# A two-block network on one core: chain step over four tiles, depthwise convolution in 32x32 diagonals, projections shifted by a slot

## What is computed

```
a, gt = jnp.split(h @ w1 + b1, 2, axis=-1)
u = a * jax.nn.sigmoid(gt)
u = causal_depthwise_conv(u, w_dw, b_dw)          # 31 taps, each channel by itself
u = jax.nn.silu(layer_norm(u, ln_g, ln_b))
return u @ w2 + b2
```

```
r = heads(lerp(0) @ w_in[0]);  k = heads(lerp(1) @ w_in[1]);  v = heads(lerp(2) @ w_in[2])
gate = lerp(3) @ w_in[3]
...
sa = jnp.einsum('dbhij,dbhj->dbhi', s, a_t)
s = s * jnp.exp(lw_t)[..., None, :] + sa[..., None] * b_t[..., None, :] + v_t[..., None] * k_t[..., None, :]
y = jnp.einsum('dbhij,dbhj->dbhi', s, r_t)
```

## Time and profile before

| | us |
|---|---|
| three runs | 2366.45, 2372.62, 2377.30 |
| median | 2372.62 |
| the profiled execution, its own time | 2365.28 |
| its span, first to last instruction | 2363.6 |
| gate of the last tile to the layer norm (convolution) | 840 to 898.5 |
| slot -1 of the scan | 1359.6 to 1436.8 |
| slots 0, 1, 2, 3 | 82.8, 93.2, 89.8, 87.5 |
| slots 4, 5, 6, 7 | 78.3, 66.6, 71.5, 57.8 |

### The profile page before, as it was taken

One profiled execution on the slowest core, in us unless ns is written; L12 is line 12 of the kernel. 1 busy time (PEld: TensorE's weight loads), 2 busy tenths in 40 slices (PEclk: granted clock), 3 DMA queues, 4 the chain that ended last, 5 costly groups with the idle time before them and its releaser, 6 DMA issues. The chain is left out here.

```text
span 2363.6 us, 39368 instructions
## 1 busy us (share of the span) xinstructions
PE 2173.4 (92%) x16594; PEld 1613.0 (68%) x16594; DVE 1015.1 (43%) x2276; ACT 526.0 (22%) x933; POOL 320.4 (14%) x530
## 2 busy tenths in 40 slices
PE   4998999999999998999998889998998899879988
PEld 3887888878888776788853355565566666436656
DVE  4643543524430572578055444534434541140262
ACT  1112122311000101100023243424434431011151
POOL 0000000000000300000005624433432120000100
PEclk8999999999999999999998989999999799899999
DMA  8543347438854320677216746545544252112100
GB/s 358 221 178 143 143 143 209 112 143 318 301 227 162 115 80 36 254 302 295 92 47 246 230 129 163 153 117 143 162 108 119 51 158 83 73 76 107 71 1 18
DMA packets 127130, 359.73 MB, mean 152 GB/s; under 512 B 78696, under 2 KB 87144, under 8 KB 109424
## 3 DMA queue, kind: packets, MB, share of 16 engines
q1 hardware_dynamic: 93776, 209.90, 25.8%
q0 software_dynamic: 32608, 146.31, 18.2%
q10 hardware_dynamic: 576, 1.05, 0.1%
HBM read 340.36 MB, written 16.85 MB: 151 GB/s over the span
## 5 line engine op out<-in xcount | busy, mean ns | idle before, releaser
L306 PE MATMUL bank<-h,ring 128*128 128x256 f32 x2304 | 501.1, 381 | 5.1 <-DVEq L1113 3.3
L306 PEld LDWEIGHTS bank<-h,ring 128*128 128x128 f32 x2304 | 439.2, 191 | 69.5 <-DVEq L1113 4.9
L1968 PE MATMUL bank<-rw_feed 128*128 128x512 f32 x464 | 248.9, 645 | 18.7 <-DMA rw_feed<-in_rkvg 8.1
L1755 POOL DMA_DIRECT2D rw_feed<-rwkv_mixes x232 | 124.8, 538 | 464.5 <-PE bank L1968 456.5
L2282 DVE TENSOR_TENSOR rw_u<-bank,rw_lam 128x128 f32<-128x128 f32 x120 | 34.9, 291 | 294.9 <-PE bank L1887 289.5
L1023 PE MATMUL bank<-ffn_hidden,ring 128*128 128x256 f32 x704 | 152.4, 379 | 3.4 <-PEq L1049 3.4
L1023 PEld LDWEIGHTS bank<-ffn_hidden,ring 128*128 128x128 f32 x704 | 133.6, 190 | 22.2 <-issue 4.1
L527 PE MATMUL bank<-h,ring 128*128 128x256 f32 x640 | 143.1, 380 | 1.1 <-PEq L323 1.1
L1968 PEld LDWEIGHTS bank<-rw_feed 128*128 128x128 f32 x464 | 77.5, 195 | 88.6 <-issue 47.7
L527 PEld LDWEIGHTS bank<-h,ring 128*128 128x128 f32 x640 | 120.2, 190 | 20.2 <-issue 4.8
L139 PE MATMUL bank<-con 128*128 128x512 f32 x220 | 103.2, 621 | 32.3 <-DVE mod L133 14.4
(11 more groups left out here) (435 smaller groups left out, 3364.7 us busy)
## 6 DMA issues: line engine op xcount, KB each, us to landing
ring<-in_stream SPq DMA_DIRECT2D x79, 2048.0 KB, 8.1
rw_feed<-rwkv_mixes POOLq DMA_DIRECT2D x232, 256.0 KB, 3.1
next_w<-in_mod_stream POOLq DMA_DIRECT2D x24, 2048.0 KB, 9.9
ctx<-in_mod_rest POOLq DMA_DIRECT2D x16, 1024.0 KB, 6.9
rw_feed<-in_rkvg POOLq DMA_DIRECT2D x232, 64.0 KB, 3.5
y<-bias_table SPq DMA_DIRECT2D x48, 128.0 KB, 4.9
rwkv_mixes<-mixed SPq DMA_DIRECT2D x6, 1024.0 KB, 3.9
rw_at<-rw_at_kept SPq DMA_DIRECT2D x16, 256.0 KB, 4.0
```

The source lines that it names most:

```text
L306: mm = pe.matmul(out, ring_tile(k, n, kt, i * P), rhs[kt], start=start and kt == kts[0], stop=stop and kt == kts[-1])
L1755: pool.dma_start(feed[:, g % FEED, 0:512], mixes[j, :, g % KT, :]).then_inc(fed[g % FEED], 16)
L1968: pe.matmul(k.psum[PROJ], feed[:, g % FEED, 512:], feed[:, g % FEED, 0:512], start=(kt == 0), stop=(kt == KT - 1)).then_inc(eaten, 1)
```

## The change

Three edits, all of them in the two stages above.

1. The convolution. PE takes four tiles (4 to 7) in place of three and DVE four in place of five. A tap is now four matmuls with 32x32 diagonals (line 1218), one for each group of 32 channels, and the group of array columns that a group's product goes to turns with the tap: `to = (g + c % 4) % 4`. Each of the four turns has its own PSUM bank. ACT copies the four banks of a tile to `turned`, and PE adds them with four 128x128 matmuls that turn the groups back (`combine`, line 1226), after which ACT adds the bias. Two identity matrices are loaded by SP at the beginning of the stage, ahead of the ring loads, and POOL waits for them before it builds its diagonals, which are four times smaller. `keep_warm` has 6 matmuls.
2. The chain step. `read_state` and `read_inner` now put head e's output into columns 64(1-e), `read_inner` is that of chunk c-2 (the other row half than `inner` of c+1), and the groups are issued direction by direction, in turn. The readout's centring matrix is turned to fit (`cen`). There are 18 items per pair (`NSTEP`).
3. The projections. Receptances and values of pairs 3 to 7 are made one slot later than before, keys of these pairs about half a slot later; the gates of pairs 0 to 3 come earlier in their slot. Slot -1 then has 8 projection matmuls (24 before), slots 0 to 3 have 32 as before, slot 4 has 24 (8 before).

```diff
-    ON_PE = (5, 6, 7)
+    ON_PE = (4, 5, 6, 7)
+    Q = 32
...
+                sp.dma_start(small_ident[:], a["small_ident"]).then_inc(idents_landed, 16)
+                for half in range(2):
+                    sp.dma_start(twice_ident[:, half * P:half * P + P], a["con"][:, CON["ident"]:CON["ident"] + P]).then_inc(
+                        idents_landed, 16)
                 load_ahead(k, sp, first, NS)
...
+                def spread_taps(n):
+
+                    i = ON_PE[n]
                     pe.wait_ge(diag_made, n + 1)
+                    if n >= 2:
+                        pe.wait_ge(convolved, n - 1)
                     for c in range(TAPS):
-                        mm = pe.matmul(k.psum[2 * n][:, 0:T], diag[:, n, c, :], u[:, i, c:c + T], start=(c == 0),
-                                       stop=(c == TAPS - 1))
-                    mm.then_inc(convolved, 1)
-                keep_warm(k, pe, 1, 16)
+                        turn = c % 4
+                        for g in range(4):
+                            to = (g + turn) % 4
+                            rows, cols = slice(Q * g, Q * g + Q), slice(Q * to, Q * to + Q)
+                            mm = pe.matmul(k.psum[4 * (n % 2) + turn][cols, 0:T], diag[rows, n, c, :], u[rows, i, c:c + T],
+                                           start=(c < 4), stop=(c >= TAPS - 4), skip_group_check=True)
+                    mm.then_inc(turned_up, 1)
+
+                def combine(n):
+
+                    pe.wait_ge(turned_down, n + 1)
+                    for turn in range(4):
+                        mm = pe.matmul(k.psum[4 * (n % 2)][:, T:2 * T], twice_ident[:, Q * turn:Q * turn + P], turned[:, n % 2, turn, :], start=(turn == 0),
+                                       stop=(turn == 3))
+                    mm.then_inc(combined, 1)
+
+                for n in range(len(ON_PE)):
+                    spread_taps(n)
+                    if n:
+                        combine(n - 1)
+                combine(len(ON_PE) - 1)
+                keep_warm(k, pe, 1, 6)
...
+                for n in range(len(ON_PE)):
+                    act.wait_ge(turned_up, n + 1)
+                    banks = k.banks[:, 2048 * (n % 2):2048 * (n % 2) + 2048].rearrange("p (r t) -> p r t", r=4)
+                    nc.scalar.copy(turned[:, n % 2, :, :], banks[:, :, 0:T]).then_inc(turned_down, 1)
+                    if n:
+                        finish(n - 1)
+                finish(len(ON_PE) - 1)
...
-                done = convolve([2, 3], done)
-                convolve([4], done)
+                convolve([2, 3], done)
...
-    keys, rows, values = (scan_project(i + 4, j) if 0 <= i + 4 < KT else [] for j in (1, 0, 2))
+    def of(n, j):
+        return scan_project(n, j) if 0 < n < KT else []
+    if i < -1:
+        return [(0.31, 0.54, of(i + 4, 1)), (0.54, 0.77, of(i + 4, 0)), (0.77, 1, of(i + 4, 2))]
     gates = scan_project(i, 3) if 0 <= i < KT else []
-    if 0 <= i < KT - 4:
-        return [(0, 0.045, keys[0:4]), (0.09, 0.36, keys[4:]), (0.36, 0.57, rows), (0.57, 0.78, values), (0.78, 0.99, gates)]
-    return [(0.04, 0.9 if KT - 4 <= i < KT - 2 else 0.3, gates), (0.31, 0.54, keys), (0.54, 0.77, rows), (0.77, 1, values)]
+    if i > KT - 4:
+        return [(0.04, 0.9 if i < KT - 2 else 0.3, gates)]
+    return [(0.02, 0.25, of(i + 3, 0) if i >= 0 else []), (0.26, 0.5, of(i + 3, 2) if i >= 0 else []),
+            (0.51, 0.74, gates), (0.75, 0.98, of(i + 4, 1))]
...
                 if c < NCK:
                     pe.wait_ge(u_done, (NCK - 1) * n + c)
-                    if c < NCK - 1:
-                        carried(n, c).then_inc(state_up, 1)
+                    for d in range(2):
+                        if c < NCK - 1:
+                            mm = carried(n, c, d)
+                            if d:
+                                mm.then_inc(state_up, 1)
+                        mm = read_state(n, c, d)
+                for d in range(2):
                     if c + 1 < NCK - 1:
-                        inner(n, c + 1)
-                    read_state(n, c)
-                read_inner(n, c - 1).then_inc(step_up, 1)
+                        mm = inner(n, c + 1, d)
+                    if c >= 2:
+                        mm = read_inner(n, c - 2, d)
+                mm.then_inc(step_up, 1)
```

## The result

The changed kernel takes 2354.22 us (median of 20 runs, 2336.53 to 2366.58) against 2368.64 us for the kernel before (20 runs, 2359.79 to 2383.61): a ratio of 0.9929, 95% interval 0.991 to 0.9948: about 17 us less by the ratio, 14 by the medians. The forecast was 2316 with a range of 2288 to 2350. The direction was right; less than a third of the gain came.

What follows compares the result with a forecast made beforehand. DVE was taken to bound the convolution, PE slots 0 to 3. Terms -22.5 (convolution), -16.5 (slots 0 to 3), -10 (slot -1), +5 (slot 4), -10.5 (slots 5 to 7) sum to -54.5: from 2370.4 to 2316 us, range 2288 to 2350.

Steps and rivals of the forecast that it cites:

- The convolution (-22.5): Convolution: DVE loses tile 4 and PE finishes its four tiles just ahead of DVE, -22.5 us.
- rival (a): Convolution: small products run four at a time or at the lower clock, +9.5 for -22.5, total 2348 us; 13%.
- the 5 us for a tile: Convolution: a tile's 248 records take 4.3 us by the nearest row's pace, taken as 5 us for record supply.
- 4 us for each us above 5.4: Convolution: once a tile takes more than 5.4 us on PE, each further us costs 4 us.
- Half of the clock: Convolution: at half clock all of PE's 33.7 us nearly doubles, so PE ends at about 900.
- The chain step (-16.5 in slots 0 to 3, -10.5 in 5 to 7): Scan: a step falls from 0.96 to 0.60 us, giving -16.5 us in slots 0 to 3 and -10.5 in 5 to 7.
- PE is the bound: Scan, slots 0 to 3: PE sets the time, busy 83.6 of 89.8 us in slot 2, 79.9 of 87.5 in slot 3.
- the tail of 14.3 us: End of a slot: DVE's serial work from `kk` to the elements takes 14.3 us, and the next slot's grams wait for it.
- The projections (-10 and, without the chain's 4, +9): Slot -1 loses 16 matmuls, -10 us; slot 4 gains 16, +5 us with the chain step's 4 us included.
- Zero while PE is the bound: Slots 0 to 3: 32 projections each stay, only their order changes, so no cost while PE sets the time.
- The clock: Scan: the forecast would be wrong if PE, no longer full, fell to the lower clock in slot -1; no size given.
- (b): Chain step: it stays at 0.96 us because the records' supply sets it, total 2349 us; 12%.

Runs made afterwards that it cites:

- experiment 1: The changed kernel again, unaltered, for a second profile: 2353.78 us at a mean clock of 0.951.
- experiment 9: The changed kernel with DVE's inverse steps laid out over 0.45 to 0.88 of a slot in place of 0.45 to 1: 2331.7 us, ratio 0.9854.
- experiment 6: The changed kernel with 64x64 diagonals in two turns in place of 32x32 in four: 2343.42 us, ratio 0.9885.
- experiment 8: The changed kernel with unused extra PE products, 12 ahead of each pair's first grams and 6 ahead of its key sums: 2338.31 us, ratio 0.9845.
- experiment 4: The kernel before with the shifted projections alone: 2371.68 us, ratio 0.9997.
- experiment 10: The kernel before with unused extra PE products, 12 ahead of each pair's first grams and 6 ahead of its key sums: 2381.52 us, ratio 1.0042.
- 14: The changed kernel with DVE's inverse steps laid out over 0.45 to 0.80 of a slot in place of 0.45 to 1: 2335.51 us, ratio 0.985.

## Why the prediction was wrong, point by point

**The convolution (-22.5).** The mechanism was right: some ten squares work at a time, rival (a)'s four did not come, and between the stops 248 records at 21 ns would make a tile of 5.3 us. The four products of a tap, which write one bank in four groups of partitions, did not go one by one: that would have been 13.4 us a tile. So Gotcha 1 of the Trainium skill's "TensorEngine Tiling (Array Packing)" does not hold here, and the estimate of 5.1 us by its "TensorE: Matmul & The Clock Gate" (packing small matmuls) agrees with the pace between the stops. The mis-sized term is the 5 us for a tile: 7.4 to 8.0 were measured, 7.8 on average (7.5 in experiment 1, where one tile with a single short stop took 5.7). The prediction's own rule, 4 us for each us above 5.4, gives -22.5 + 4 x 2.4 = -12.9, and the stage measured 45.7 - 58.4 = -12.7. It had named the cause ("records must also be supplied for 20 us on end") and allowed 0.7 us for it; the row it scaled from, 64 records in 1.10 us, is shorter than the 128 records after which the stop comes. Half of the clock, which it had only as a case for the whole stage, came for 3.4 to 6.8 us at the first stop, in all nine profiles with 32x32 and in none of the four with 64x64. Some 3 us that were not counted came back at the layer norm, which now starts at the full clock. The part alone gave -21 with an interval of -13 to -28.

**The chain step (-16.5 in slots 0 to 3, -10.5 in 5 to 7).** The step's 0.60 was measured as 0.63 (in slot 2 of the kernel before most steps took 1.05 us, not the 0.96 of the earlier trace rows). PE's busy time in slots 0 to 3 fell by 331.1 - 316.1 = 15 us, close to the forecast. But the slots gave 7.9 us (345.4 for 353.3) in the fastest execution and were 5.7 longer in the typical one. The step of the argument that failed is "PE is the bound" in these slots. In the fastest execution 7 of the 15 us came back as idle time of PE, 29.3 us for 22.2; in the typical one PE was busy for 330.6 us, so the lower clock took the whole saving. Only half of what lies behind the spread had been discounted; the tail of 14.3 us in the earlier trace rows was in fact the end of the slot, with 3 us of PE idle before each slot's first grams, and experiment 9 gives back more than half of that wait. The prediction had named this tail as what would make it wrong, as it had the clock, but its sum has no price for it beyond that half. In slots 5 to 7 the profiled execution has 186.0 us for 195.9, the -10 of the forecast. That is luck in part: at its clock of 0.94 the term came out, but other profiles with the same chain step and nearly the same work there have 191.7 us (experiment 1, at 0.90), 195.7 (experiment 6, 0.88) and 201.5 (experiment 8, 0.86).

**The projections (-10 and, without the chain's 4, +9).** Alone they gave -9 in slot -1 (61.4 for 70.3), +10 in slot 4 and nothing in the total, 0.9997: the terms were right. "Zero while PE is the bound" held for the shift alone as well, 352.9 us for 353.3 in slots 0 to 3, although the first grams already waited (experiment 4). What it left out is that the same waits stand in slots which the shorter step no longer fills. In the whole change slot 4 lost 12 us (90.5 for a forecast of 83.5), at a clock of 0.87 and with 8.0 us of waiting for DVE at its end, where it was 5.2. Slot -1 gave 4.9 us in the fastest execution and 8.9 in the typical one. With extra products the two took 60.8 and 86.6 (experiment 8), but without them 61.4 and 84.8 in experiment 6, so single executions do not show that the products helped there.

**The clock.** The prediction named a fall to 1.2 GHz as what would make it wrong, but for slot -1 alone and without a price. That is the second failed step: the terms of slots 0 to 3 were made from slots at 0.99 to 1.00, as if the clock were given. Removing PE's work opened waits of 1.3 and 2.9 us, in or after which the level fell in the typical execution; slots of 85.9 became 92. Filling these waits kept slots 0 to 3 at the full clock (experiment 8), and the same filling brought nothing in the kernel before, whose first grams wait for at most 1.3 us in these slots (experiment 10). Between the fastest and the median execution of the changed kernel lie 18 us.

**The sum.** By stage, in us, the profiled executions of the kernel before (2365.28), of the changed kernel (2336.53, its fastest) and of experiment 1 (2353.78, a typical one):

| | before | fastest | typical | forecast of the change |
|---|---|---|---|---|
| start to slot -1, convolution in it | 1366.5 | 1347.5 | 1345.1 | -22.5 |
| slot -1 | 70.3 | 65.4 | 61.4 | -10 |
| slots 0 to 3 | 353.3 | 345.4 | 359.0 | -16.5 |
| slot 4 | 78.3 | 90.5 | 90.5 | +5 |
| slots 5 to 7 | 195.9 | 186.0 | 191.7 | -10.5 |
| rest | 299.3 | 299.8 | 304.1 | 0 |

Up to the end of slot -1 the change brings 24 and 30 us of the 32.5 that were forecast. From slot 0 on it brings 5 us in the fastest execution and loses 18.5 in the typical one, for 22 that were forecast. The parts alone gave -21, -16 and -1 for -22.5, -31 (slot 4's 4 included) and -1; then some 20 us were lost between them. Rivals (a) and (b), 2348 and 2349, come nearest by the number, but neither happened: some ten products ran at a time, and the step went to 0.63. A rival "PE's savings in slots 0 to 3 are given back to DVE's tail and to the clock" was missing; with the -12.9 of the convolution it would have come to 2370.4 - 12.9 - 10 + 9 - 10.5 = 2346, less whatever slots 0 to 3 keep.

**What stays open.** Why the bonus waits 1.5 us and the key sums 1.3 us in the new order was not tried. Neither was a shorter path from the decay's sums by ACT's exponentials to the elements, which is what ends the tail in experiments 9 and 14. The falls of the clock in slots 4 to 7 were not worked on either. And which execution keeps the clock in a place where another loses it is not explained by anything in these traces.

## What to carry to other kernels

When work is taken from the engine that is busy all the time, look for the serial piece of another engine that its work was covering, and move that piece in the same change: here one line of DVE's order was worth as much as the whole change had brought, 18 us by the ratios against 17. Price a stream of small matmuls by its instructions as well as by the array: if it is longer than what the rows show without a stop, the fewer and larger ones may be faster although the array needs twice the time for each tile. And put a price on the lower clock wherever a change opens a wait of some us on PE in a stretch that was full.

## What the runs showed of the hardware

A long stream of small products is held up by the supply of its instructions. With 32x32 products at 21 ns a record, each stop ends 1.2 to 1.6 us after a transfer of 16 KB on the instruction queue, and stops stand only at steps of 128 records. Not each step has one: at the lower clock (845 to 852 us in experiment 1) PE runs through them. With 64x64 at 57 ns a record there is none.

The granted clock fell in or right after the first stop of that stream, 2.7 to 3.4 us, in all nine profiles, and after waits as short as 1.3 us with 2-column products behind them, but then not every time. And the mean clock is no measure of speed between kernels: the slowest kernel of the study had the highest, 0.968 to 0.972, since busy work that nobody needs raises it too.
